# Output projection of a hybrid attention and retention layer: seven block products for eight

## Chip, core and metric

The kernel runs on one core of one Trainium2 chip. The metric is the device time of one execution in microseconds (us). The engines are named as in the profile: PE (TensorE, matmuls), PEld (its weight loads), DVE (VectorE), ACT (ScalarE), POOL (GpSimd) and SP (SyncE, which issues nearly all DMAs).

## What is computed

```python
h = rms_norm(x, norm_gain)                       # x: 1 x 2048 x 1024
proj = jnp.einsum('bsd,de->bse', h, w_in)        # 1024 -> 5632 columns
aq, ak, av, ag, rq, rk, rv, rg = jnp.split(proj, SPLIT_POINTS, axis=-1)
attn = window_attention(aq, ak, av, q_gain, k_gain, sinks)
ret = retention(rq, rk, rv, ret_norm_gain)
mixed = jnp.concatenate([attn * silu(ag), ret * silu(rg)], axis=-1)
x = x + jnp.einsum('bse,ed->bsd', mixed, w_out)  # 2048 -> 1024 columns
```

All matrices are float32. The last line is the output projection, and it is the part of which this document tells.

## The kernel before

**Units.** The rows are cut into four blocks of 512 and the heads into four groups. One group in one block is a unit n, from 0 to 15. Each unit has "jobs", each of which fills one PSUM bank. There are three job banks, taken in turn, so a job may start when the job three before it has been read out (`bank_free`, L1410).

- Q jobs 0 to 3 make query, key and value for a tile of 128 rows each (384 columns, 24 matmuls).
- G jobs 4 to 7 make the attention gate, and the retention's query and key (512 columns, 24 matmuls each).
- V jobs 8 to 11 make the retention's value and gate (512 columns, 24 matmuls each).
- O jobs 12 to 19 are the output projection: four row tiles t by two halves h of 512 output columns, each over the unit's 512 mixed features (four slices k of 128). A job has 4 x 3 = 12 matmuls of 128x128 on 512 columns, since every operand is a pair of a rounded high and a low part, and high x high, high x low and low x high are summed (L1469 to L1471). The O jobs of unit n-1 run inside unit n, between its Q and G jobs. In the last unit they stand behind V(15), and those of unit 15 at the very end.

Between jobs PE runs the small attention and retention steps: TQ, S_, PT, PV, A, I and MT. MT(n,t) transposes the finished retention tile; `mth` on ACT (L696) and `mtl` on DVE (L910) write its high and low part. `mixh` on ACT and `mixl` on POOL (L421) do that for the attention tile. `add` on DVE (L1152) adds each O job's bank to `acc`, which starts as x and is stored at the end of each block. The retention tile itself goes through `gna` and `gnv` (DVE L1111 to L1121), a power on POOL (L435), `gnm` (DVE L1125), `gnx` (ACT L569) and `gnb` (DVE L1132).

**Weights.** They stand in two buffers of 8 x 512 columns, a high one (wH) and a low one (wL). Four panels (Q, G, V, O) go through them in turn, each in four chunks of two k slices. In the first four units a chunk is loaded into a staging buffer, ACT copies it rounded (`wh1`, L541), POOL subtracts (`wl1`, L396), and SP saves both parts to DRAM. The other 12 units reload both parts, a whole panel at a time, as soon as the panel two before it is used up (SP L254).

**Order.** Each engine has its own list of calls written out by hand, and works in order. Nothing is reordered on the chip.

## Time and profile before

| | us |
|---|---|
| median of 3 runs | 1573.88 |
| lowest and highest | 1573.47 and 1574.04 |
| span of the profiled execution | 1571.6 |
| PE busy in it | 1552.0 |
| DVE, ACT, POOL busy | 1124.6, 833.3, 457.9 |

The span runs from the first to the last instruction of one profiled execution. The median is 2.3 us above it, so a change worked out on the span is set off against 1571.6 us, and 2.3 us are put on again for the time. PE is busy in 99% of the span, so first its work counts, then what makes it wait. Its matmuls overlap in the records: one is recorded as 0.39 us long, while the next begins 0.23 us after it.

### The profile page before, as it was taken

What the parts mean: (1) busy time and instruction counts of PE and PEld (TensorE: products, weight loads), DVE (VectorE), ACT (ScalarE), POOL (GpSimd) and SP (SyncE); (2) the same over time, 40 slices, a digit from 0 to 9 for tenths busy, and PEclk for the clock granted to TensorE, in tenths of its full rate; (3) what the DMA queues carried; (4) which work ended last, traced back from release to release, by engine and by line L of the source; (5) the groups of instructions that cost most, each with busy time, mean ns of one, the idle gap of its engine ahead of it and who ended that gap; (6) DMA issues with size and microseconds to landing.
All of it is one profiled execution on the core that took longest, in us unless ns stands there. A gap on an engine that the chain in (4) does not pass through costs nothing.

```text
span 1571.6 us, 24771 instructions
## 1 busy us (share of the span) xinstructions
PE 1552.0 (99%) x8120; PEld 1355.1 (86%) x8120; DVE 1124.6 (72%) x2874; ACT 833.3 (53%) x2331; POOL 457.9 (29%) x453
## 2 busy tenths in 40 slices
...
PEclk9999999999999999999999999999999999999999
...
GB/s 319 308 287 310 155 334 215 269 210 212 296 258 197 161 177 183 165 236 125 215 206 208 250 140 186 211 97 249 172 158 281 146 207 191 140 191 137 174 212 54
DMA packets 123327, 323.65 MB, mean 206 GB/s; under 512 B 16832, under 2 KB 60224, under 8 KB 123200
## 3 DMA queue, kind: packets, MB, share of 16 engines
...
q14 instruction: 61, 0.50, 0.1%
...
## 4 chain that ended last, share of the span: by engine, by line
PE 92%; DVE 4%; POOL 1%; DMA 1%; issue 1%; ACT 1%; SPq 0%; DVEq 0%; ACTq 0%; POOLq 0%
PE jb L1469 26%; PE jb L1470 26%; PE jb L1471 26%; PE ob L1528 2%; PE s L1504 2%; PE ptb L1513 2%; PE ob L1488 1%; PE s L1567 1%; PE ab L1578 1%; PE s L1566 1%; POOL wL L396 1%; PE s L1405 1%; DMA stage<-wp_dram 1%; PE ab L1405 0%; PE ab L1407 0%
## 5 line engine op out<-in xcount | busy, mean ns | idle before, releaser
L1469 PE MATMUL jb<-wH,hTH 128*128 128x512 f32 (+1 forms) x1024 | 376.3, 367 | 13.0 <-POOL wL L396 10.7
L1470 PE MATMUL jb<-wL,hTH 128*128 128x512 f32 (+1 forms) x1024 | 372.6, 364 | 0.0
L1471 PE MATMUL jb<-wH,hTL 128*128 128x512 f32 (+1 forms) x1024 | 372.3, 364 | 0.0
L1469 PEld LDWEIGHTS jb<-wH,hTH 128*128 128x128 f32 x1024 | 193.0, 188 | 33.6 <-POOL wL L396 12.4
L1471 PEld LDWEIGHTS jb<-wH,hTL 128*128 128x128 f32 x1024 | 193.1, 189 | 20.4
L1470 PEld LDWEIGHTS jb<-wL,hTH 128*128 128x128 f32 x1024 | 193.3, 189 | 17.9
L1469 PE MATMUL jb<-wH,mxH 128*128 128x512 f32 x512 | 207.1, 405 | 0.9 <-ACT rawqn L550 0.6
L1469 PE MATMUL jb<-hTH,wH 128*128 128x512 f32 x512 | 201.4, 393 | 0.0
L1471 PE MATMUL jb<-wH,mxL 128*128 128x512 f32 x512 | 200.6, 392 | 0.0
L1470 PE MATMUL jb<-wL,mxH 128*128 128x512 f32 x512 | 200.5, 392 | 0.0
L1470 PE MATMUL jb<-hTL,wH 128*128 128x512 f32 x512 | 200.0, 391 | 0.0
L1471 PE MATMUL jb<-hTH,wL 128*128 128x512 f32 x512 | 199.7, 390 | 0.0
L599 ACT ACTIVATE sx<-sx,nm 128x128 f32<-128x128 f32 x256 | 99.8, 391 | 166.1 <-DVE d L1001 166.0
L421 POOL TENSOR_TENSOR mxL<-mixr,mxH 128x256 fp32r<-128x256 f32 x64 | 48.8, 762 | 449.8 <-ACT mxH L661 449.1
L396 POOL TENSOR_TENSOR wL<-stage,wH 128x512 fp32r<-128x512 f32 (+1 forms) x126 | 159.5, 1291 | 63.8 <-ACT wH L541 63.7
L403 POOL TENSOR_TENSOR rstd<-ms,mhalf 128x5 f32<-128x5 f32 x64 | 75.9, 1186 | 134.3 <-DVE ms L943 134.2
L1471 PEld LDWEIGHTS jb<-wH,mxL 128*128 128x128 f32 x512 | 96.2, 188 | 21.1
L1471 PEld LDWEIGHTS jb<-hTH,wL 128*128 128x128 f32 x512 | 96.2, 188 | 20.5
L1469 PEld LDWEIGHTS jb<-hTH,wH 128*128 128x128 f32 x512 | 96.3, 188 | 18.9 <-ACT rawqn L550 0.3
L1469 PEld LDWEIGHTS jb<-wH,mxH 128*128 128x128 f32 x512 | 96.4, 188 | 18.2 <-ACT rawqn L550 0.8
L1470 PEld LDWEIGHTS jb<-hTL,wH 128*128 128x128 f32 x512 | 96.3, 188 | 18.3
L1470 PEld LDWEIGHTS jb<-wL,mxH 128*128 128x128 f32 x512 | 96.6, 189 | 16.6
...
## 6 DMA issues: line engine op xcount, KB each, us to landing
wH<-scrH SPq DMA_DIRECT2D x144, 512.0 KB, 7.0
wL<-scrL SPq DMA_DIRECT2D x144, 512.0 KB, 7.9
stage<-wp_dram SPq DMA_DIRECT2D x48, 512.0 KB, 6.7
scrH<-wH SPq DMA_DIRECT2D x48, 512.0 KB, 6.9
scrL<-wL SPq DMA_DIRECT2D x48, 512.0 KB, 7.8
...
out_dram<-acc SPq DMA_DIRECT2D x16, 512.0 KB, 3.0
```

The source lines that it names most:

```text
L396: pool.tensor_tensor(wL[b][:, s, 0:w], stage_of(at // 2, w)[:, s % 2], wH[b][:, s, 0:w].bitcast(F32), ALU.subtract).then_inc(S["s_wl"], 1)
L403: pool.tensor_tensor(rstd[:, t % 2], ms[:, t % 2], mhalf[:, 0:5], ALU.pow).then_inc(S["s_rstd"], 1)
L421: pool.tensor_tensor(mxL[:, 0:2, cols], mixr[:, :, :], mxH[:, 0:2, cols].bitcast(F32), ALU.subtract).then_inc(S["s_mixl"], 1)
L599: act.activation(v, v, ACT.Exp, bias=nm4[:, t % 2, i:i + 1], accum_out=den[:, t % 2, i:i + 1])
L1405: pe.matmul(o, lh, rh_, start=i == 0, stop=False)
L1469: pe.matmul(o, lh, rh_, start=i == 0, stop=False)
L1470: pe.matmul(o, lh, rl_, start=False, stop=False)
L1471: m = pe.matmul(o, ll, rh_, start=False, stop=i == last)
L1488: m = pe.transpose(tr[:, c * P:(c + 1) * P], qn[:, t % 2, c * P:(c + 1) * P], ident[:, :])
L1504: m = pe.matmul(s_parts[:, par, hp], qS[:, t % 2, 2 * hp + par], kHL[:, :, win], start=True, stop=True)
L1513: m = pe.transpose(ptb[:, i * P:(i + 1) * P], sx[:, at:at + P], ident[:, :])
L1528: m = pe.matmul(o, v, pT[:, par * 256:(par + 1) * 256].rearrange("p (r q) -> p r q", q=64), start=i == 0, stop=i == 1)
```

## The change

**Seven products.** The O work of a unit is a product of two 2 x 2 block matrices: rows 0 to 255 and 256 to 511, against features of attention and retention, against columns 0 to 511 and 512 to 1023. The change forms it by seven block products P1 to P7 in place of eight, and sums of blocks before and after. A product has two halves of 128 rows, and each half is one job of two k slices, that is 6 matmuls. There are 14 O jobs a unit (12 to 25), 84 matmuls in place of 96. P2, P4 and P3 go on in the bank in which P1, P5 and P7 stand.

**Sums of the mixed operand.** POOL and ACT form four more operands a unit out of the mixed tiles (now kept as mix0 and mix1): s3a, s3l, s1l, s2a, s2l, s4a (two instructions) and s4l on POOL, each 512 columns; sh 1 to 4 on ACT. `mixh` and `mixl` are left for two of four tiles. DVE adds the turned retention tile into mix1 (L1392) for two tiles a unit.

**Sums of the weights.** In the first four units DVE forms four sums of weight blocks (`wtw`, 1024 columns each) and three low parts (`wld`), and POOL four low parts (`wlo`). The O panel so has seven chunks of 1024 columns where it had four.

**Output.** acc is changed by two subtractions before (`ini`) and two behind (`fin`) in each block, on POOL, 1024 columns each; in the last block `fiz` on DVE does the second, in four parts of 512. There are 14 `add` a unit for 8. Stores and refills of acc move from SP's queue to ACT's, but for the last block's stores.

**Other moves.** The weights go chunk by chunk through a ring of seven places (a Q panel takes three); a place is loaded when its chunk's last matmul is done, and raw weights land in the low ring itself. O jobs come in pairs between the Q and G jobs. For blocks 1 to 3, `xl` (8 a block, 512 columns) moves from DVE to POOL.

Jobs of a middle unit n, where the two digits are product and half of unit n-1; before, all eight O jobs stood between Q3 and G0:

```diff
+WOVEN = "Q0 Q1 10 11 Q2 20 21 Q3 50 51 G0 40 41 G1 70 71 G2 30 31 G3 60 61 V0 V1 V2 V3".split()
+CARRIED = {2: 1, 4: 5, 3: 7}
+OPERAND = {1: 0, 2: 1, 4: 2, 5: 0, 6: 3, 7: 4, 3: 1}
+OUT_CHUNK = {1: 0, 2: 1, 5: 2, 6: 3, 4: 4, 7: 5, 3: 6}
...
+    tail = [(0, 1, 0), (0, 1, 1), (0, 6, 0), (0, 2, 0), (0, 2, 1), (0, 6, 1), (0, 5, 0), (0, 5, 1), (0, 7, 0), (0, 4, 0), (0, 4, 1),
+            (0, 3, 0), (0, 7, 1), (1, 1, 0), (1, 1, 1), (0, 3, 1), (1, 2, 0), (1, 2, 1), (1, 5, 0), (1, 5, 1), (1, 6, 0), (1, 4, 0),
+            (1, 4, 1), (1, 7, 0), (1, 7, 1), (1, 6, 1), (1, 3, 0), (1, 3, 1)]
...
 def job(n, j):
-                    t, h = (j - J_OUT) // 2, (j - J_OUT) % 2
-                    pairs = [((mxH[:, k, cols], mxL[:, k, cols]), (W[:, 4 * h + k, :], L[:, 4 * h + k, :]))
-                             for k in range(4)]
+                    prod, half = product_of(j)
+                    name, value = {1: ("s_mixl", nth(n, 2, half)), 2: ("s_mtl", nth(n, 4, half)), 4: ("s_mtl", nth(n, 4, 2 + half)),
+                                   5: ("s_s1l", n + 1), 6: ("s_s2l", n + 1), 7: ("s_s3l", n + 1), 3: ("s_s4l", n + 1)}[prod]
+                    pe.wait_ge(S[name], value)
+                    pairs = [((mxH[:, at, half, k], mxL[:, at, half, k]), (hi(chunk)[:, k], lo(chunk)[:, k])) for k in range(2)]
...
 def mth(n, t):
-                    act.wait_ge(S["s_job"], JOB_DONE[n - 1, J_OUT + 2 * t + 1])
+                    act.wait_ge(S["s_job"], product_done(n - 1, 3 if t < 2 else 4))
...
+            def ini(b, i):
+                if b:
+                    pool.wait_ge(s_ai[3], 16 * b)
+                    pool.wait_ge(s_ai[1 + i], 16 * b)
+                else:
+                    pool.wait_ge(S["s_xsq"], NT)
+                    for t in range(2 * (1 - i), NT):
+                        pool.wait_ge(s_first[t], 16)
+                difference(i, S["s_ini"])
```

POOL's order from the start. wL is `wl1`, xr and rstd are powers for the norms. Before:

```order
L396 TENSOR_TENSOR wL<-stage,wH 128x384 x6
L396 TENSOR_TENSOR wL<-sx,wH 128x384 x2
L396 TENSOR_TENSOR wL<-stage,wH 128x512
L441 TENSOR_TENSOR xr<-xm,mhalf 128x2
L396 TENSOR_TENSOR wL<-stage,wH 128x512 x6
L441 TENSOR_TENSOR xr<-xm,mhalf 128x2 x2
L403 TENSOR_TENSOR rstd<-ms,mhalf 128x5
```

And now:

```order
L560 TENSOR_TENSOR wL<-wraw,wH 128x384 x8
L685 TENSOR_TENSOR xr<-xm,mhalf 128x2
L577 TENSOR_TENSOR rstd<-ms,mhalf 128x5
L685 TENSOR_TENSOR xr<-xm,mhalf 128x2 x2
L560 TENSOR_TENSOR wL<-wraw,wH 128x512
L577 TENSOR_TENSOR rstd<-ms,mhalf 128x5
L560 TENSOR_TENSOR wL<-wraw,wH 128x512
L649 TENSOR_TENSOR acc<-acc 128x2x512
L560 TENSOR_TENSOR wL<-wraw,wH 128x512 x2
L685 TENSOR_TENSOR xr<-xm,mhalf 128x2
L560 TENSOR_TENSOR wL<-wraw,wH 128x512 x4
```

The first G panel's subtractions now stand behind two powers for the first tile, and six of the eight behind the subtraction on acc (`ini`), which waits until ACT has squared all four row tiles.

DVE's order in unit 2, where the O jobs of unit 1 are added. Before:

```order
L1152 TENSOR_TENSOR acc<-acc,jb 128x512
L1132 SCALAR_TENSOR_TENSOR oraw<-oraw,xr,gg 128x256
L1152 TENSOR_TENSOR acc<-acc,jb 128x512
L956 TENSOR_TENSOR rawqn<-rawqn,rstd 128x320
L959 TENSOR_TENSOR rawqn<-rawqn,rstd 128x64
L968 SCALAR_TENSOR_TENSOR qS<-ob,qkg,qS 64x4x64 x2
```

And now:

```order
L1403 TENSOR_TENSOR wraw<-stage 128x1024
L1408 TENSOR_TENSOR stage<-stage,wraw 128x1024
L1410 TENSOR_TENSOR stage<-stage 128x1024
L1430 TENSOR_TENSOR acc<-acc,jb 128x512
L1392 TENSOR_TENSOR mix<-mix,ab 128x256
L1153 TENSOR_TENSOR mxL<-ab,mxH 128x256
L348 TENSOR_TENSOR wL<-wraw,wH 128x1024
L1430 TENSOR_TENSOR acc<-acc,jb 128x512
L1212 SCALAR_TENSOR_TENSOR qS<-ob,qkg,qS 64x4x64 x2
L1217 SCALAR_TENSOR_TENSOR kHL<-ob,qkg,kHL 128x128
L1413 TENSOR_TENSOR stage<-stage 128x1024
```

Five instructions of 1024 columns stand among the additions and the attention's steps, where there were none.

POOL's order at the end. mxL is the low part of an O operand, gnf the power in the last retention tile's norm. Before:

```order
L435 TENSOR_TENSOR gnf<-ve,mhalf 128x2
L421 TENSOR_TENSOR mxL<-mixr,mxH 128x2x128
L435 TENSOR_TENSOR gnf<-ve,mhalf 128x2
L421 TENSOR_TENSOR mxL<-mixr,mxH 128x2x128 x2
L105 UNCONDITIONAL_BRANCH
```

And now:

```order
L603 TENSOR_TENSOR mxraw<-mix 128x512
L608 TENSOR_TENSOR mxL<-mxraw,mxH 128x512
L679 TENSOR_TENSOR gnf<-ve,mhalf 128x2
L621 TENSOR_TENSOR mix<-mix 128x512
L613 TENSOR_TENSOR mxL<-mix,mxH 128x512
L626 TENSOR_TENSOR mxL<-mix,mxH 128x512
L634 TENSOR_TENSOR mix<-mix,mxH 128x512
L637 TENSOR_TENSOR mix<-mix,mxL 128x512
L642 TENSOR_TENSOR mxL<-mix,mxH 128x512
```

Behind the last power stand six instructions of 512 columns; L613 is `s1l`, for which PE's P5 of unit 15 waits, and `s2a` (L621) stands ahead of it.

## Rows read from the trace of the kernel before

**Rows 1.** The page of the profile: span, busy time, PE clock in tenths
```profile
span 1571.6 us, 24771 instructions
PE 1552.0 (99%) x8120; PEld 1355.1 (86%) x8120; DVE 1124.6 (72%) x2874; ACT 833.3 (53%) x2331; POOL 457.9 (29%) x453
PEclk9999999999999999999999999999999999999999
```

**Rows 2.** Windows by unit (0, 1, 2, 8, last): length, busy us, clock, DMA share, GB/s
```profile
59.80:162.46 102.66, 100.41 (x534) 87.36 (x533) 91.36 (x201) 67.67 (x188) 63.80 (x56) 1.00 0.75 270
162.46:259.65 97.19, 97.19 (x514) 85.10 (x513) 76.14 (x182) 60.05 (x159) 59.71 (x55) 1.00 0.69 259
259.65:356.79 97.14, 97.14 (x514) 85.10 (x513) 75.49 (x172) 58.42 (x155) 57.24 (x52) 1.00 0.59 215
842.45:938.75 96.30, 96.30 (x506) 84.28 (x505) 64.33 (x173) 49.46 (x144) 17.47 (x19) 1.00 0.49 180
1491.54:1571.60 80.06, 76.25 (x380) 64.11 (x378) 45.26 (x116) 25.02 (x68) 10.97 (x14) 1.00 0.35 132
```

**Rows 3.** Waits of PE over the span: total us, times, longest
```profile
PE jb L1469 <- POOL wL L396: 10.7, 3, 9.9
PE jb L1469 <- DVE hTL L910: 2.2, 2, 1.9
```

**Rows 4.** Timeline of PE, O jobs at the end: start, length; first and last of 60
```profile
1554.03 0.39 PE L1469 MATMUL jb<-wH,mxH 128*128 128x512 f32 x1
...
1567.41 0.39 PE L1471 MATMUL jb<-wH,mxL 128*128 128x512 f32 x1
```

**Rows 5.** Groups by shape: busy us, mean ns of one, idle before
```profile
L396 POOL TENSOR_TENSOR wL<-stage,wH 128x512 fp32r<-128x512 f32 x96 | 127.6, 1355 | 52.8 <-ACT wH L541 52.8
...
L1152 DVE TENSOR_TENSOR acc<-acc,jb 128x512 f32<-128x512 f32 x128 | 87.4, 683 | 25.9 <-PE jb L1471 24.4
...
L910 DVE TENSOR_TENSOR mxL<-ab,mxH 128x256 fp32r<-128x256 f32 x64 | 26.7, 418 | 0.2
...
L696 ACT ACTIVATE mxH<-ab 128x256 fp32r<-128x256 f32 x64 | 23.8, 371 | 23.8 <-PE ab L1578 23.8
```

**Rows 6.** Two DVE groups of one size by tile: ns min/median/max
```profile
L910 DVE TENSOR_TENSOR hTL<-xt,hTH x30: 678/685/1766, 17.9 to 1168.3; 128x512 fp32r<-128x512 f32 x30
...
L910 DVE TENSOR_TENSOR pTL<-ptb,pTH x64: 678/684/693, 64.3 to 1538.1; 128x512 fp32r<-128x512 f32 x64
```

**Rows 7.** DMA issues: size, median us from issue to landing
```profile
wL<-scrL SPq DMA_DIRECT2D x144, 512.0 KB, 7.9
stage<-wp_dram SPq DMA_DIRECT2D x48, 512.0 KB, 6.7
...
out_dram<-acc SPq DMA_DIRECT2D x16, 512.0 KB, 3.0
```

**Rows 8.** Timeline of PE at the start: jobs 2, 3 and 4
```profile
26.54 0.34 PE L1469 MATMUL jb<-wH,hTH 128*128 128x384 f32 x1
...
29.09 0.41 PE L1469 MATMUL jb<-wH,hTH 128*128 128x384 f32 x1 [1.88 <-DVE hTL L910]
...
33.52 0.50 PE L1469 MATMUL jb<-hTH,wH 128*128 128x512 f32 x1
```

**Rows 9.** Timeline of DVE at the end: a retention tile's norm, the last addition
```profile
1531.40 0.23 DVE L1121 TENSOR_SCALAR ve<-mv,xe 128x2 f32<-128x2 f32 x1
...
1533.62 0.49 DVE L1132 SCALAR_TENSOR_TENSOR oraw<-oraw,xr,gg 128x256 f32<-128x256 f32 x1 [0.34 <-ACT oraw L569]
...
1534.75 0.42 DVE L1111 TENSOR_TENSOR oraw<-oraw,s 128x256 f32<-128x256 f32 x1
...
1536.01 0.23 DVE L1121 TENSOR_SCALAR ve<-mv,xe 128x2 f32<-128x2 f32 x1
...
1567.83 0.69 DVE L1152 TENSOR_TENSOR acc<-acc,jb 128x512 f32<-128x512 f32 x1 [2.03 <-PE jb L1471]
```

More of the change, by code:

```diff
@@ new lines, in ring_places @@
+def ring_places():
+    free, places = [0] * SLOTS, []
+    for n, p, c in CHUNKS:
+        size = 2 * W_WIDTH[p]
+        if p == 0 and c:
+            places.append((places[-1][1], places[-1][1] + size))
+        elif p == 0:
+            at = min(range(SLOTS - 2), key=lambda i: (max(free[i:i + 3]), i))
+            free[at:at + 3] = [last_use((n, p, 3))] * 3
+            places.append((1024 * at, 1024 * at + size))
+        else:
+            at = min(range(SLOTS), key=lambda i: (free[i], i))
+            free[at] = last_use((n, p, c))
+            places.append((1024 * at, 1024 * at + size))
+    return places
@@ new lines, with released @@
+EARLY_AT = {k: i for i, k in enumerate(EARLY)}
+def released(chunk):
+    n, p, c = chunk
+    if p == 3:
+        return "s_job", max(JOB_DONE[n, OUT_JOB[i, q]] for i in OUT_CHUNK if OUT_CHUNK[i] == c for q in range(2))
+    if c < 3:
+        return "s_rel", EARLY_AT[chunk] + 1
+    return "s_job", JOB_DONE[n, PANEL_LAST[p]]
+PLAIN = [k for k in CHUNKS if k[0] < NU and k[1] < 3]
+PLAIN_AT = {k: i for i, k in enumerate(PLAIN)}
+RAW = [k for k in CHUNKS if k[0] < NU and (k[1] < 3 or k[2] in (1, 6))]
@@ L195, in build @@
         s_w = [S["s_w0"], S["s_w1"], S["s_w2"]]
+        s_rw = [S[f"s_rw{i}"] for i in range(LANES)]
         s_xt = [S["s_xt0"], S["s_xt1"]]
@@ new lines, in s4l, with difference @@
+            def s4l(n):
+                pool.wait_ge(S["s_s4h"], n + 1)
+                pool.tensor_tensor(flat(mxL[:, 1]), flat(mix1[:, :, :, :]), flat(mxH[:, 1]).bitcast(F32), ALU.subtract
+                                   ).then_inc(S["s_s4l"], 1)
+            def difference(i, done):
+                left, right = acc[:, :, 0:512], acc[:, :, 512:1024]
+                to = left[:, 2:4] if i == 0 else right[:, 0:2]
+                pool.tensor_tensor(to, right[:, 2:4], to, ALU.subtract).then_inc(done, 1)
@@ new lines, in _ @@
+            s4a(11); s4l(11); rql(12); mixl(12, 0); rkl(12); mixl(12, 1); fin(2, 0); fin(2, 1); ggm(12, 0); s3a(12)
+            s3l(12); ggm(12, 1); ini(3, 0); ini(3, 1); gpow(12, 0); ggm(12, 2); gpow(12, 1); ggm(12, 3); rpow(13, 0)
+            gpow(12, 2); rpow(13, 1); gpow(12, 3); s2a(12); s1l(12); rpow(13, 2); s4a(12); s2l(12); s4l(12)
+            rpow(13, 3); mixl(13, 0); rql(13); mixl(13, 1); rkl(13); ggm(13, 0); s3a(13); s3l(13); ggm(13, 1)
+            gpow(13, 0); ggm(13, 2); gpow(13, 1); ggm(13, 3); gpow(13, 2); rpow(14, 0); rpow(14, 1); gpow(13, 3)
@@ new lines, in quarter, with rows_of, store @@
+            def quarter(whole, q):
+                return whole[:, 2 * (q % 2):2 * (q % 2) + 2, q // 2 * 512:q // 2 * 512 + 512]
+            def rows_of(whole, b, q):
+                at = b * BLK + q % 2 * 2 * P
+                return whole[0, at:at + 2 * P, q // 2 * 512:q // 2 * 512 + 512].rearrange("(t p) d -> p t d", p=P)
+            def store(b, q):
+                last = NU * b + NU - 1
+                if q in (0, 3):
+                    act.wait_ge(S["s_acc"], added(last, (2,) if q == 0 else (1, 5, 6, 7)))
+                else:
+                    act.wait_ge(S["s_fin"], 2 * b + q)
+                act.dma_start(rows_of(out, b, q), quarter(acc, q)).then_inc(s_st[q], 16)
```

1554 lines of the change are left out of this document (868 added, 686 removed).

## The prediction

> **What bounds the kernel now.** I read the page first: PE is busy 1552.0 of 1571.6 us at full clock [rows 1]. Then the windows by unit: from unit 1 on PE is busy in the whole of each window, while DVE fills 76.14 of 97.19 us in unit 1 and 64.33 of 96.30 in unit 8 [rows 2]. Then PE's waits: 10.7 us on POOL's wL and 2.2 on hTL [rows 3], both in the first 30 us, and nothing worth naming later. So the middle is bound by PE's own work. Matmuls taken out count in full there, and waits put in count too, because there are none to hide behind.
>
> **What is removed.** 12 matmuls of 512 columns in each of 16 units, 192 in all. A record's length (0.39 us) overlaps the next, so the price is the spacing: 60 matmuls in a row start from 1554.03 to 1567.41, 13.38 us in 59 steps, 0.2268 us each [rows 4]. 192 x 0.2268 = **43.5 us** off, 2.72 a unit. Six matmuls make a job of 1.36 us. A job starts in that same spacing, so six more jobs a unit cost PE nothing by these rows. All terms below are PE's waits, put on again.
>
> **The end: +7.5.** This is the term I trust most, since the order has nothing between. P3 of unit 14 reads its operand where `mth` for tiles 0 and 1 of unit 15 must write. P3's last half, job(14,23), now stands behind P1 of unit 15, and right behind it PE has MT(15,1).
> - MT(15,1) needs the bank of MT(15,0) read: `mth` 0.37 and `mtl` 0.42 after job(14,23) [rows 5]. PE idles 0.9 us with a hop.
> - MT(15,3) needs the last tile's norm. ACT copies that tile only behind `mth` of tile 1: 0.37 + about 0.37 for the copy (of `mth`'s size), then 1.26 from `gna` to `ve` (1534.75 to 1536.01) and 2.71 from `ve` to the end of `gnb` (1531.40 to 1534.11) [rows 5, 9], 4.7 us. PE has two jobs and a transpose of about 0.25 for it, 3.0. It idles 1.7, with DVE's additions in between about 2.
> - P5 of unit 15 stands right behind MT(15,3) and waits for `mth` 0.37, the addition 0.42, `s2a` 1.36 and `s1l` 1.36 [rows 5], with four hops 3.9.
> - Behind the last matmul comes `add` and now a `fiz` of 0.68 [rows 5, 9]: 0.7.
> Sum 7.5, and 5 to 10 as its bounds. `s4l` has 8 jobs, 10.9 us, for six POOL and ACT steps; it hides.
>
> **The start: +2.** Job 2 ends at about 27.1 (its last three matmuls start at 26.54 [rows 8]). Then ACT evicts (1.3) and squares the fourth tile (1.05), and `ini` runs 2 x 1.355: until 32.2. POOL then has two low parts (2.7), the power that the transposes XB ahead of job 4 wait for (0.7): 35.6. Four more low parts end at 41.0, and job 4 with them at 41.5, where it started at 33.52 and took 5.5 [rows 8], so ended at 39.1. XB's and TQ's 0.9 us came after that. So 1.5 to 2.4 late. Bounds: 0, as POOL was late there already [rows 3], and 6 if both `ini` count.
>
> **Units 1 to 3: +9.** Two things come together, counted once.
> - DVE: 75.5 us of unit 2 are filled [rows 2]. To it come 6 `add` (4.1), 2 additions for mix1 (0.84) and 7 instructions of 1024 columns at twice 0.684 (9.6) [rows 5, 6]: 90.0 of a unit of 97.14 - 2.72 = 94.4. POOL's load grows from 57 to about 71 (8 + 8 more instructions' worth less what goes), and with 40 us more of POOL work DVE's same 172 instructions took 11 us longer than in unit 8 [rows 2], so 14 more give 3.8: 93.8, or 99%. At 89% in unit 0 PE lost 2.25 us [rows 2], at 78% in unit 1 nothing.
> - V panel: its first place comes free 12.2 us before V0 (G3, four O jobs and A). Loading takes 6.7 by the median, 3.0 by the store that has the queues to itself [rows 7], ACT 0.6, then POOL eight low parts, one of rk and a `mixl`, 12.9: ready 8.0 or 4.3 us after V0 starts, where its last slice is wanted at 4.8. So 0 to 3.2 us.
> I take 3 us in each of three units. The bounds are 0 and 6.5 a unit, the latter for a DVE that reaches 93%: 93.8 / 0.93 = 100.9.
>
> By the Trainium skill (SBUF — State Buffer, Who interferes with whom) a DVE instruction with two SBUF inputs and a GpSimd instruction that reads SBUF exclude each other for a whole instruction. That speaks against this change, which gives both more of them. The trace agrees: hTL with two SBUF inputs ranges from 678 to 1766 ns, pTL with one in PSUM only from 678 to 693 [rows 6]. By the rule each of the seven new ones could wait out one low part of 1355 ns, up to 9.5 us a unit more; the sum with 9.5 in place of 3 in three units would be some 19 us above mine.
>
> **The other units: +1.5.** The ACT, POOL and DVE work grows, but DVE has 32 us idle in unit 8 and POOL 79 [rows 2], and some 5 and 9 us are added. The tightest chain is MT(n,3), `mth`, addition, `s2a`, `s1l`, then P5: 3.9 us beside a P2 half, Q3 and S_, 6.1 us, of which DVE's and ACT's queues take some. Banks: the job behind a pair has 2.7 us for the eviction of the one before it, 0.7 on DVE or 0.6 on ACT. Block changes put `fin` and `ini`, 10.8 us, on POOL. Bounds 0 and 12. No gain is possible from the moved `xl` or refills, since PE waits for none of them now.
>
> **The sum.** 1571.6 - 43.5 + 7.5 + 2 + 9 + 1.5 = 1548.1 of span, and with 2.3 around it **1550.4**; I say 1550.
>
> **Rivals.**
> - *The covers hold* (0.20). Only the end costs: 1571.6 - 43.5 + 7.5 + 2.3 = 1538. For it: PE never waited in units 1 and 2 at 78% DVE. Against it: 95 to 99% is another matter.
> - *DVE and POOL bound the first block* (0.20). 6.5 us a unit in place of 3, and 3 more in unit 0 or 4: 1550 + 13.5 = 1564. By the skill's lock above it would be more, to 1569.
> - *The ring's leads fail in every later unit* (0.06): slower than before. The last G chunk of a unit takes the place of a Q chunk that is free at half of Q3. To its use are left 12 matmuls of Q (2.1), two O jobs (2.7), 18 of G (4.1) and two small steps (0.9): 9.8 us, the last V chunk about the same. The panel before had a whole panel's time. wL lands 7.9 us after issue by the median [rows 7], with the issue 8.4, so 1.4 is left. Loads that come 3 us later lose 1.6 at two or three places, and with the raised traffic (a unit reloads 18.9 MB for 15.7, three O chunks more) maybe 2 at each: 5.5 a unit, 66 in 12 units, 1616. It decides from 1.9 us a unit, that is from landings of some 10.3. Against it: 7.9 is for eight issued in a burst, here they come in pairs, and DMA is busy only 49% [rows 2].
> - *Short products gain less* (0.04). If each O job cost 0.1 us at its head, 96 more jobs cost 10: 1560.
>
> **How the numbers follow.** The forecast has 0.50, with a range of its own of 1543 to 1558. A measurement tells about 0.2%, 3.1 us, from no change. Slower than 1577.0 is only the ring's case: 0.05. Within: 0.02 from the thin ends of the rivals. Faster: 0.93. The range from 1536 to 1566 takes in the first two rivals and the short products, about 0.85.
>
> **What would show it.** PE's records must fall by 192 and a middle unit last 93.6 us, not 96.3. PE must wait for `s1l` (POOL mxL L613) once by about 4 us some 18 us before the end, and for the acc subtraction's successors near 35 us. Units 1 to 3 would last about 97, and DVE be at 93% or more there. Wrong it would be if middle units stay above 95, with PE waiting for DMA wH or wL (the ring), or if units 1 to 3 last 94.4 (the covers hold) or over 100.

## The result

The kernel after the change takes 1643.17 us (median of 4 runs, 1641.58 to 1645.9), the kernel before 1573.68 beside it: a ratio of 1.0443, with a 95% interval of 1.0428 to 1.0458. It is 69.5 us slower, where 1550 and a gain had been forecast. The matmuls went away as planned, 192 of them. In the profiled execution, the longest of the four (1645.9 us, a span of 1643.9), the kernel is 72.3 us behind, so 115.8 us of new loss stand against 43.5 us saved; by the medians it is 113.0.

The page of the kernel after, in the lines that answer to [rows 1]:

```profile
span 1643.9 us, 25336 instructions
PE 1548.5 (94%) x7928; PEld 1333.7 (81%) x7928; DVE 1321.2 (80%) x3010; ACT 866.0 (53%) x2359; POOL 678.2 (41%) x571
PEclk9999999999999999999999999999999999999998
```

PE was busy in 99% of the span and is so in 94%. DVE's busy time has grown by 197 us, POOL's by 220. By the prices of the forecast DVE's new instructions come to about 100 us (14.5 us in each of four units and 4.9 in the other twelve, less 16 for `xl`). The mean granted clock is 0.984 of full.

Where the time went is read best by stretches that hold the same jobs in both kernels. Units are cut at the first matmul of Q0. Windows of the kernel after, with the columns of [rows 2]: unit 0, units 1 to 4, units 5 to 14, unit 15 with the end:

```profile
9.33:98.24 88.91, 81.00 (x402) 69.70 (x402) 79.03 (x158) 57.46 (x151) 58.74 (x49) 0.96 0.75 286
98.24:540.23 441.99, 397.95 (x1993) 338.37 (x1992) 390.77 (x753) 236.59 (x604) 263.88 (x197) 0.97 0.71 260
540.23:1511.65 971.42, 951.21 (x4947) 825.35 (x4946) 753.91 (x1864) 510.37 (x1437) 315.22 (x283) 1.00 0.59 216
1511.65:1643.87 132.22, 118.31 (x593) 100.24 (x591) 92.31 (x230) 56.42 (x159) 35.84 (x34) 0.97 0.54 197
```

And the same stretches before:

```profile
9.89:88.43 78.54, 74.59 (x372) 63.27 (x372) 66.41 (x138) 54.80 (x145) 54.87 (x48) 1.00 0.88 329
88.43:483.62 395.19, 393.27 (x2085) 344.24 (x2083) 310.76 (x733) 229.82 (x615) 198.24 (x180) 1.00 0.66 244
483.62:1446.56 962.94, 962.94 (x5044) 842.53 (x5043) 664.26 (x1785) 490.86 (x1407) 183.49 (x198) 1.00 0.51 186
1446.56:1571.60 125.04, 121.23 (x628) 105.03 (x626) 79.07 (x214) 54.19 (x158) 19.88 (x22) 1.00 0.42 155
```

Take the length before, less 2.72 us for each unit's removed matmuls (none in unit 0, which has no O work yet, and 5.4 in the last stretch, which has that of two units), from the length after. The loss is 9.8 us up to unit 1, counted from the start of the span, **57.7 in units 1 to 4**, **35.7 in units 5 to 14** and 12.7 in unit 15 and the end. (The counts show that up to 44 short matmuls, some 5 us, changed sides at a cut, so the first and third loss are a little too large and the second too small.)

No single wait stands out. PE's waits over the whole span, in us, times and longest (compare [rows 3]):

```profile
PE jb L1737 <- DVE hTL L1463: 9.3, 1, 9.3
PE jb L1737 <- issue: 8.7, 3, 3.5
PE ob L1758 <- DVE kHL L1217: 8.3, 7, 2.4
PE ab L1848 <- DVE oraw L1382: 6.7, 7, 2.9
PE ptb L1783 <- DVE sx L1254: 6.0, 7, 1.6
PE jb L1737 <- DVE acc L1430: 5.2, 2, 2.8
PE ab L1859 <- POOL xr L685: 4.6, 1, 4.6
...
PE jb L1737 <- POOL wL L560: 3.4, 6, 1.1
PE jb L1737 <- DMA wL<-scrL: 3.4, 4, 1.5
```

Only the first is the start-up that the kernel before had too (9.9 us there, put down to POOL's wL). Most others name DVE, each time another of its results, and each is 1 to 3 us long. That is the picture of an engine that is late as a whole.

**Why DVE is late.** Two stretches of the same 6 us in unit 2. First POOL, then DVE (start, length):

```profile
246.36 1.30 POOL L634 TENSOR_TENSOR mix<-mix,mxH 128x512 f32<-128x512 f32 x1
247.73 1.29 POOL L637 TENSOR_TENSOR mix<-mix,mxL 128x512 f32<-128x512 f32 x1
248.98 1.29 POOL L626 TENSOR_TENSOR mxL<-mix,mxH 128x512 fp32r<-128x512 f32 x1
250.23 2.39 POOL L348 TENSOR_TENSOR wL<-stage,wH 128x1024 fp32r<-128x1024 f32 x1
```

```profile
247.29 0.69 DVE L1240 TENSOR_REDUCE m<-sx 128x4 f32<-128x512 f32 x1
248.01 1.03 DVE L1243 SCALAR_TENSOR_TENSOR nm<-m,nsink 128x4 f32<-128x4 f32 x1
249.07 1.22 DVE L1245 TENSOR_TENSOR d<-nm,sink 128x4 f32<-128x4 f32 x1
250.21 0.48 DVE L1186 TENSOR_REDUCE ss<-th 128x5 f32<-128x320 f32 x1
250.72 1.93 DVE L1187 TENSOR_SCALAR ms<-ss 128x5 f32<-128x5 f32 x1
```

nm, d and ms work on 4 or 5 columns and take 0.16, 0.16 and 0.17 us at their shortest. Here each ends when the POOL instruction beside it ends: nm at 249.04 (POOL 249.02), d at 250.29 (250.27), ms at 252.65 (252.62). The two TENSOR_REDUCE are not stretched. Three of POOL's added instructions turned 0.5 us of DVE's work into 4.2. The same by tile: aL (128x256, two SBUF inputs), shortest, median and longest in ns, before and after ([rows 6] had hTL):

```profile
L910 DVE TENSOR_TENSOR aL<-amr,aH x64: 410/419/1505, 77.4 to 1528.0; 128x256 fp32r<-128x256 f32 x64
```

```profile
L1153 DVE TENSOR_TENSOR aL<-amr,aH x64: 409/419/2617, 77.3 to 1590.1; 128x256 fp32r<-128x256 f32 x64
```

For the whole kernel I add up, over all DVE instructions, the length less the shortest of the same line and shape, and call that the **excess**. It was 95 us before and is 212 after: 51 and 99 in units 1 to 4, 23 and 85 in units 5 to 14. (Finer or coarser groups of shapes move each of these by up to 6 us.) Not all of the growth lies beside POOL's new instructions: `rqL`, which POOL formed before too, now stands beside DVE's `mix` (64x256), 14 of 80 of which take over 0.9 us in units 5 to 14 where it was 2, some 11 us of excess.

**The clock.** In unit 2, timeline of PE (start, length), and then windows around it (the granted clock is the last figure but two):

```profile
278.67 0.39 PE L1739 MATMUL jb<-wH,mxL 128*128 128x512 f32 x1
282.31 0.30 PE L1810 MATMUL ab<-ident,kr 128*128 128x128 f32 x1 [3.26 <-issue]
...
284.61 0.63 PE L1737 MATMUL jb<-wH,mxH 128*128 128x512 f32 x1
285.03 0.63 PE L1738 MATMUL jb<-wL,mxH 128*128 128x512 f32 x1
...
287.08 0.39 PE L1737 MATMUL jb<-wH,mxH 128*128 128x512 f32 x1
```

```profile
274.00:278.60 4.60, 4.60 (x27) 4.01 (x27) 4.50 (x16) 4.11 (x14) 2.50 (x4) 1.00 0.99 380
...
283.00:287.00 4.00, 4.00 (x13) 3.25 (x14) 3.92 (x6) 2.62 (x11) 4.00 (x4) 0.57 1.02 418
```

PE stood for 3.26 us, and for the next 4 us its matmuls came every 0.43 us in place of 0.23, at 0.57 of the full clock, near the lower of its two levels (1.2 GHz). Behind the start-up there are seven waits of 2.5 us or more, and six of them lie in or right beside such a stretch; other stretches follow groups of shorter waits. By the spacing, the matmuls in them cost 17.9 us over full speed in the whole kernel; the same count gives 2.5 before, where the clock was full up to the last matmul. PE is busy for 46.2 us at the low level, half of which, 23 us, is the most that it can have cost. So some 15 to 23 of the 115.8 us, an estimate, are not waits but what waits cause.

The rest is waiting: PE's idle time grew from 19.6 to 95.4 us, in 88 waits for 10. Each wait also hides some 0.16 us behind the recorded end of the matmul before it (0.39 us long at a spacing of 0.23), which makes another 12 us by estimate.

### The profile page after: what moved, and what is told of

It is laid out like the page before. It is cut to its first block, busy times and chain, and to the rows that moved or that the text cites. A ratio compares the mean times of both kernels' runs of the same rounds, so it can differ in the third digit from the quotient of the medians.

```text
span 1643.9 us, 25336 instructions
## 1 busy us (share of the span) xinstructions
PE 1548.5 (94%) x7928; PEld 1333.7 (81%) x7928; DVE 1321.2 (80%) x3010; ACT 866.0 (53%) x2359; POOL 678.2 (41%) x571
## 4 chain that ended last, share of the span: by engine, by line
PE 47%; DVE 15%; issue 4%; DMA 2%; ACT 1%; POOL 1%; SPq 0%; DVEq 0%; POOLq 0%; ACTq 0%
PE jb L1737 14%; PE jb L1738 13%; PE jb L1739 13%; DMA wL<-scrL 2%; PE ob L1798 1%; DVE acc L1430 1%; DVE aL L1153 1%; DVE rst L1352 1%; PE ptb L1783 1%; DVE rst L1153 1%; PE s L1774 1%; DVE oraw L1359 1%; DVE qS L1212 1%; PE s L1836 1%; DVE kwL L1153 1%
## 5 line engine op out<-in xcount | busy, mean ns | idle before, releaser
L1737 PE MATMUL jb<-wH,hTH 128*128 128x512 f32 (+1 forms) x1024 | 376.9, 368 | 10.4 <-DVE hTL L1463 9.3
L1737 PE MATMUL jb<-wH,mxH 128*128 128x512 f32 x448 | 186.9, 417 | 20.1 <-issue 8.7
L1738 PE MATMUL jb<-wL,mxH 128*128 128x512 f32 x448 | 179.6, 401 | 0.0
L1739 PE MATMUL jb<-wH,mxL 128*128 128x512 f32 x448 | 179.2, 400 | 0.0
L1430 DVE TENSOR_TENSOR acc<-acc,jb 128x512 f32<-128x512 f32 x224 | 152.4, 681 | 21.8 <-PE jb L1739 18.4
L560 POOL TENSOR_TENSOR wL<-wraw,wH 128x512 fp32r<-128x512 f32 (+1 forms) x96 | 124.6, 1319 | 44.2 <-ACT wH L756 43.9
L1737 PEld LDWEIGHTS jb<-wH,mxH 128*128 128x128 f32 x448 | 86.6, 193 | 37.0 <-issue 17.1
L584 POOL TENSOR_TENSOR rqL<-th,rqH 64x512 fp32r<-64x512 f32 x32 | 42.4, 1326 | 179.1 <-ACT zst L854 162.1
L679 POOL TENSOR_TENSOR gnf<-ve,mhalf 128x2 f32<-128x2 f32 x64 | 47.9, 748 | 163.9 <-DVE ve L1371 163.9
L1738 PEld LDWEIGHTS jb<-hTL,wH 128*128 128x128 f32 x512 | 96.7, 189 | 19.2
```

The costliest lines, as they stand in the source:

```text
L560: pool.tensor_tensor(lo(chunk)[:, s % 2], raw_lo(chunk)[:, s % 2], hi(chunk)[:, s % 2].bitcast(F32), ALU.subtract).then_inc(S["s_wl"], 1)
L584: pool.tensor_tensor(rqL[rows, a], th[rows, :], rqH[rows, a].bitcast(F32), ALU.subtract).then_inc(S["s_rql"], 1)
L679: pool.tensor_tensor(gnf[:, t % 2, 0:2], ve[:, :], mhalf[:, 0:2], ALU.pow).then_inc(S["s_grs"], 1)
L1430: v.tensor_tensor(a, a, bank_of(n, J_OUT + i)[:, :], ALU.add).then_inc(S["s_acc"], 1)
L1737: pe.matmul(o, lh, rh_, start=begins and i == 0, stop=False, **go_on)
L1738: pe.matmul(o, lh, rl_, start=False, stop=False, **go_on)
```

## The experiments

Theory A: POOL's added instructions read SBUF and stretch DVE's. Rival B: the ring and the order of the jobs. Rival C: DVE's own added instructions. Rival D: what was added holds POOL's queue, and what stands behind it is late. All kernels made from the kernel after stand side by side. Medians are of two or three runs each (four of the kernel after); single runs of one kernel differ by 0.5 to 8 us, the two of sums_filled by 14. The losses are those of the profiled run, by the stretches above, in us; that run was the slower one in some, 1616.8 us in sums_filled and 1600.9 in all_pool_paced.

| kernel | median us | ratio to before, 95% | to unit 1 | 1 to 4 | 5 to 14 | 15, end | excess 1 to 4 | 5 to 14 |
|---|---|---|---|---|---|---|---|---|
| after the change | 1643.2 | 1.0443 (1.0428 to 1.0458) | 9.8 | 57.7 | 35.7 | 12.7 | 99 | 85 |
| sums_filled | 1609.8 | 1.0231 (1.0125 to 1.0337) | 9.3 | 44.6 | 22.6 | 10.3 | 78 | 50 |
| weight_sums_filled | 1603.3 | 1.0190 (1.0160 to 1.0219) | 8.6 | 18.0 | 32.3 | 13.7 | 65 | 102 |
| both_filled | 1591.6 | 1.0116 (1.0083 to 1.0148) | 7.4 | 21.0 | 24.3 | 11.0 | 53 | 65 |
| reload_half | 1636.1 | 1.0396 (1.0366 to 1.0427) | 8.4 | 55.6 | 28.2 | 12.7 | 96 | 87 |
| ini_fin_short | 1631.8 | 1.0370 (1.0330 to 1.0409) | 7.7 | 51.6 | 27.0 | 12.8 | 94 | 80 |
| adds_half | 1632.1 | 1.0371 (1.0341 to 1.0401) | 9.2 | 51.3 | 29.7 | 11.9 | 94 | 87 |
| pool_low_filled | 1623.7 | 1.0321 (1.0291 to 1.0351) | 9.1 | 33.5 | 36.3 | 12.8 | 73 | 88 |
| pool_low_paced | 1623.7 | 1.0317 (1.0287 to 1.0347) | 10.0 | 40.0 | 29.7 | 13.0 | 76 | 82 |
| dve_weight_filled | 1630.8 | 1.0367 (1.0337 to 1.0397) | 10.8 | 41.1 | 37.4 | 13.2 | 92 | 103 |
| sums_paced | 1615.7 | 1.0266 (1.0236 to 1.0295) | 8.3 | 42.0 | 21.8 | 12.2 | 72 | 46 |
| sums_on_dve | 1662.8 | 1.0565 (1.0527 to 1.0603) | 8.6 | 57.7 | 55.4 | 13.2 | 97 | 50 |
| low_on_dve | 1644.0 | 1.0446 (1.0415 to 1.0476) | 9.2 | 56.5 | 36.0 | 13.4 | 74 | 82 |
| all_pool_paced | 1594.9 | 1.0145 (1.0112 to 1.0178) | 8.7 | 29.6 | 19.2 | 13.3 | 49 | 37 |
| pool_paced_dve_filled | 1588.9 | 1.0106 (1.0086 to 1.0126) | 5.8 | 21.5 | 21.7 | 13.9 | 48 | 54 |
| all_short | 1563.8 | 0.9943 (0.9921 to 0.9966) | 5.8 | 8.9 | 10.4 | 8.5 | 53 | 66 |

The last column can't be compared for the five kernels in which DVE's weight sums are filled. There a few additions of units 1 to 3 take 0.62 us in place of 0.67 to 0.69, and as the shortest of their kind they lift the excess of all others. Counted from the fastest tenth of each kind, units 5 to 14 have 81 us in the kernel after and 23 in the kernel before, and 78 in weight_sums_filled, 44 in both_filled, 81 in dve_weight_filled, 33 in pool_paced_dve_filled and 43 in all_short.

**sums_filled.** The eight instructions for the operand sums become fills of the same tiles, for example:

```diff
 def s1l(n):
     pool.wait_ge(S["s_s1h"], n + 1)
-    pool.tensor_tensor(flat(mxL[:, 0]), flat(mix1[:, :, :, :]), flat(mxH[:, 0]).bitcast(F32), ALU.subtract
+    pool.memset(flat(mxL[:, 0]).bitcast(F32), 0.0001
                        ).then_inc(S["s_s1l"], 1)
```

> The kernel after the change, but the eight instructions of POOL that form the sums of the mixed operand and their low parts only write a constant over the same tiles, and read nothing; every wait and every other instruction stays. (The sums are left out, so the products are of other numbers.) Theory A, POOL's reading of SBUF stretches DVE's instructions with two SBUF inputs, and DVE's late results stop PE: the time that DVE's instructions take over the shortest of their kind falls from 4 to 12 us a unit to about 3 in units 5 to 14, these units lose 2 to 3 us less each, units 1 to 4 some 2 to 4 less, and the kernel takes 1595 to 1615 us in place of 1643. Rival B, the order of jobs and the ring of weights make PE wait: nothing of that changes, 1635 to 1643. Rival C, only DVE's own added instructions matter: these are all still there, 1635 to 1643 too, but with DVE's excess down.

1609.8 us, 33 less, in the range of theory A; its two runs, 1602.8 and 1616.8, lie on both sides. In the profiled one, the slower, units 1 to 4 and 5 to 14 gained 13 us each, and the excess fell in both.

**weight_sums_filled** and **both_filled.** The same for `wtw`, `wld` and `wlo`; then both edits.

```diff
-    v.tensor_tensor(t1, b12, b11, ALU.subtract).then_inc(S["s_twin"], 1)
+    v.memset(t1, 0.01).then_inc(S["s_twin"], 1)
...
-    return engine.tensor_tensor(lo(chunk), src, hi(chunk).bitcast(F32), ALU.subtract)
+    return engine.memset(lo(chunk).bitcast(F32), 0.00001)
```

> The kernel after the change, but the four sums of weights a unit, and the seven low parts of the output weights (three on DVE, four on POOL), only write a constant, in units 0 to 3; waits stay. (The weight sums and those low parts are left out.) They are 8.5 us of DVE and 10.8 us of POOL in each of four units. Theory A or C (DVE is full in the first five units, 91 to 93 percent): units 1 to 4, which last 108.2, 111.7, 109.4 and 112.8 us, come to 98 to 103, and the kernel to 1605 to 1615. Rival B (the V panel's chain, the order and the ring): units 1 to 4 keep at least 105, 1630 or more. Units 5 to 15 must not change under any theory.

> Both edits of the two runs before together (sums of operands and of weights and their low parts only write constants). Theory A: the two gains add or do better, 1560 to 1580, with units 1 to 3 near 97 and units 5 to 14 near 94. Rival C: as the weight sums alone, 1605 to 1615. Rival B: 1625 or more, and then what is left of PE's waits names the place.

The weight sums cost 40 us, nearly all of it in units 1 to 4; 1603.3 is 2 us below the range of theories A and C. Both together gave 52 and not 73: 1591.6 is above what I gave to theory A and below all that I gave to the others. The two overlap in units 1 to 4, and some 60 us of loss do not come from either.

**Three other loads, one at a time.** reload_half, ini_fin_short and adds_half:

```diff
-    sp.dma_start(dst.bitcast(F32), src[:, c]).then_inc(s_ld[i % LANES], 16)
+    sp.dma_start(dst[:, 0].bitcast(F32), src[:, c, 0]).then_inc(s_ld[i % LANES], 16)
```

```diff
-    pool.tensor_tensor(to, right[:, 2:4], to, ALU.subtract).then_inc(done, 1)
+    pool.tensor_tensor(to[:, :, 0:32], right[:, 2:4, 0:32], to[:, :, 0:32], ALU.subtract).then_inc(done, 1)
```

```diff
-    v.tensor_tensor(a, a, bank_of(n, J_OUT + i)[:, :], ALU.add).then_inc(S["s_acc"], 1)
+    v.tensor_tensor(a[:, 0:256], a[:, 0:256], bank_of(n, J_OUT + i)[:, 0:256], ALU.add).then_inc(S["s_acc"], 1)
```

> The kernel after the change, but each reload of a chunk in units 4 to 15 brings only the first of its two k slices, half of the bytes, through the same waits. (The second slice keeps older weights.) Rival B, the ring's leads are too short: PE's waits for DMA wL (3.4 us in all by the trace) and what follows them vanish, and more than that if late weights also hide behind other waits, 5 us or more off in units 5 to 14, 1620 to 1638. Theory A (DVE is late, the ring is only touched): at most 4 us off, 1638 to 1643.

> The kernel after the change, but the subtractions on acc at the start and end of each block (ini and fin on POOL) cover 32 of 512 columns. (Most of acc is so not prepared.) They are 2.7 us of POOL each, two before block 0 and four at each of three block changes. Theory D, they hold POOL's queue: the 4.6 us that PE waits for the first tile's power near 34 us fall to 1 or less, and with it 3 to 5 us of the start; units 4, 8 or 9, 12 or 13 lose 1 to 4 us less each; 1625 to 1636. If the start is late by POOL's low parts anyway: 1640 to 1643.

> The kernel after the change, but each of the 14 additions a unit covers 256 of its bank's 512 columns. (Half of the output is not added.) DVE so spends 14 x 0.27 = 3.8 us less a unit, less than the eight additions cost before the change. An addition reads one operand from PSUM. Theory C, the count and length of DVE's instructions matter: 3 to 4 us less in each of units 1 to 4 and 1 to 2 in the others, 1610 to 1625. Theory A, the stretching by POOL matters more than the own load: units 5 to 14 gain under 1 us each, units 1 to 4 gain 2 to 3, 1625 to 1637.

Halved reloads gave 7 us, so rival B is true, but small. The low parts of the weights land 7.4 us after issue in the kernel after, by the median ([rows 7]: 7.9):

```profile
wL<-scrL SPq DMA_DIRECT2D x180, 512.0 KB, 7.4
```

PE's four waits for DMA wL (3.4 us) lie in units 4, 6, 7 and 10, three of them at an O job behind the first G job. The short ini and fin gave 11 us, 2 of them at the start and the rest around the block changes, and the halved additions 11, spread over all units, as theory A had it.

**What POOL's added work costs the kernel before.** It got eight more POOL instructions a unit in units 6 to 15, for which nobody waits:

```diff
+    def extra():
+        pool.tensor_tensor(more[:, 512:1024], more[:, 0:512], more[:, 0:512], ALU.subtract).then_inc(S["s_mhalf"], 1)
...
-    ...; rpow(6, 2); gpow(5, 3); rpow(6, 3); xpow(2, 0); xpow(2, 1)
+    ...; rpow(6, 2); extra(); extra(); extra(); extra(); extra(); extra(); gpow(5, 3); rpow(6, 3); xpow(2, 0); xpow(2, 1)
```

> The kernel before the change, and in units 6 to 15 eight more instructions of POOL a unit, 512 columns with two SBUF inputs, two behind the second gg and six behind the third rstd, where the changed kernel has its operand sums; no other engine waits for them (result unchanged). Theory A: DVE's excess over the shortest instruction of each kind rises from 2.2 us a unit to 5 to 9 there, with DVE's own count the same; PE has slack for most of it in this kernel, so 0 to 10 us more in all. A price per instruction of POOL of 0.4 to 0.8 us of DVE comes out. If POOL and DVE do not hinder each other: DVE's busy time in units 6 to 14 stays within 0.5 us, and the kernel's time too.

It took 1596.5 us (ratio 1.0147, 1.0117 to 1.0176), 22.9 more than the kernel before, where I had given 0 to 10. The excess rose by only 2 us a unit, and theory A's row of 5 to 9 us did not come. PE's waits tell which power was late, the fourth one of `rpow`, which now stood behind six instructions:

```profile
PE ob L1500 <- DVE kHL L985: 17.2, 18, 1.3
```

The next kernel has the six behind that power.

```diff
-    ...; rpow(6, 2); extra(); extra(); extra(); extra(); extra(); extra(); gpow(5, 3); rpow(6, 3); xpow(2, 0); xpow(2, 1)
+    ...; rpow(6, 2); gpow(5, 3); rpow(6, 3); extra(); extra(); extra(); extra(); extra(); extra(); xpow(2, 0); xpow(2, 1)
```

> The kernel before the change with the same eight more POOL instructions a unit as in the run named before_pool_sums, which cost 22.9 us though no engine waits for them, but the six of them stand behind the last rstd power of a unit in place of ahead of it. If they cost by POOL's queue (the power for the fourth tile's key and query is late, so kHL is, for which PE waited 17.2 us there): 1574 to 1577. If they cost by stretching DVE: 1585 to 1597 as before. DVE's excess should be 4 us a unit in both cases.

1575.8 us (ratio 1.0014, 1.0003 to 1.0025), with the same excess, and the row is

```profile
PE ob L1500 <- DVE kHL L985: 1.9, 2, 1.0
```

That is rival D, pure: the same instructions cost 22.9 us at one place of POOL's queue and 2.3 us at another. Then eight instructions a unit on DVE were added as well, one of their places being:

```diff
+    def more_dve():
+        link(v.tensor_tensor(more[:, 1024:1536], more[:, 0:512], more[:, 0:512], ALU.subtract))
...
-    ...; part2(7, 0); tql(7, 2); ...
+    ...; part2(7, 0); more_dve(); tql(7, 2); ...
```

> The kernel before the change with the eight POOL instructions a unit of the run before_pool_sums_later, and in units 6 to 15 eight more instructions on DVE too, 512 columns with two SBUF inputs, one behind each of the four softmax steps and one behind each mixing step; no other engine waits for any (result unchanged). Both engines then carry in units 6 to 14 more than in the changed kernel (DVE 74 to 80 us at its shortest against 69 to 77). If load and contention are what cost the changed kernel 3.6 us a unit there: units of 98 to 101 us, 1595 to 1620. If it is rather where things stand in the queues and the ring: under 1 us a unit, 1575 to 1585.

1580.3 us (ratio 1.0041, 1.0022 to 1.0061), 6.9 more, 0.7 a unit, where the kernel after loses 3.6 a unit. But its load is not that of the kernel after. In units 6 to 14 DVE's own work, its busy time less the excess, is 68.9 us a unit and 67.0 in the kernel after, so it has a little more; POOL is busy for 27.0 us and not 31.9, ACT for 49.0 and not 51.3, the excess is 5.0 and not 9.0, and nobody waits for what was added. The run shows that DVE's own work alone does not explain units 5 to 14. It does not part the order from the contention and from the chains that pass through the new instructions.

**Stretching or queue, in the kernel after.** First one half of the weight sums at a time.

```diff
+    if c not in LOW_ON_DVE:
+        return engine.memset(lo(chunk).bitcast(F32), 0.00001)
     return engine.tensor_tensor(lo(chunk), src, hi(chunk).bitcast(F32), ALU.subtract)
```

> The kernel after the change, but the four low parts of weight sums that POOL forms in each of units 0 to 3 only write a constant; DVE's seven instructions stay. (Those low parts are left out.) Both kinds together gave 40 us. If the stretching of DVE by POOL's reads is what fills DVE (theory A), this half gives 12 to 25 us, with DVE's excess in units 1 to 4 down by 3 or more each: 1618 to 1631. If it is DVE's own instructions and their place in its queue (theory C), at most 8: 1635 to 1643.

> The kernel after the change, but the four sums and three low parts of weights that DVE forms in each of units 0 to 3 (1024 columns each) only write a constant; POOL's four low parts stay. (Those sums are left out.) Theory C: this half gives 28 to 40 of the 40 us of both, 1603 to 1615. Theory A: 15 to 28, 1615 to 1628.

POOL's four low parts a unit (16 in all, about 2.4 us each) cost 19.5 us, DVE's 28 instructions only 12.4: the first is in theory A's range, the second 3 us above it. So DVE's own work is the smaller part of what the weight sums cost. The fills are shorter than the sums (0.96 us for 1024 columns), so this does not yet tell theory A from rival D. The two runs named paced do. There each sum is filled two and a half times over, so that POOL is held as long, and reads nothing:

```diff
-    out_low(pool, n, c).then_inc(S["s_olp"], 1)
+    low = lo((n, 3, c)).bitcast(F32)
+    out_low(pool, n, c)
+    pad(low)
+    pad(low)
+    pool.memset(low[:, 0], 0.00001).then_inc(S["s_olp"], 1)
```

> As the run pool_low_filled (POOL's four low parts of weight sums a unit, in units 0 to 3, only write constants; 20 us faster), but each now writes its constant two and a half times over, so that it holds POOL for the 2.4 us that the low part took, and reads nothing. If the 20 us came from POOL's reads stretching DVE (theory A), they stay: 1620 to 1628. If they came from POOL's queue (powers and low parts of weights behind them came earlier): 1638 to 1645.

> As the run sums_filled (the eight operand sums and low parts a unit on POOL only write constants; 33 us faster), but each writes for the 1.3 us that the sum took, and reads nothing. Theory A: the 33 us stay but for the few of the end's chain, 1608 to 1618. POOL's queue (in the kernel before, six more instructions ahead of one power cost 23 us, behind it 2): most of them go, 1630 to 1643.

(Here `out_low` only waits.) The low parts: 1623.7 us with short fills and 1623.7 with long ones. The operand sums: 1609.8 and 1615.7. So by medians of two runs each the 19.5 us and some 27 of the 33 us come from POOL's reads. In the stretch of units 1 to 4 the split is less clean (24 us off with short fills, 18 with long ones), and the 6 us between 1609.8 and 1615.7 are less than sums_filled differs from itself. Then everything that POOL was given was made long fills (sums, low parts, ini and fin, hTL of blocks 1 to 3), and after that DVE's weight sums fills too:

> The kernel after the change with all that it gave POOL replaced by constants written for as long as the work took, reading nothing: the operand sums, the four low parts of weight sums, ini and fin, and the eight hTL of blocks 1 to 3. (All of these are left out.) POOL's busy time and queue stay, DVE's instructions too. The sums alone gave 27 us, the low parts 20. Theory A (reads stretch DVE): 1643 less 47 less 5 to 15 for the rest, 1580 to 1592, and DVE's excess in units 5 to 14, 4 to 12 us, near 1 to 3. If POOL's queue at the block changes (ini, fin) cost the rest: 1592 to 1600.

> The run before, and DVE's four weight sums and three low parts a unit in units 0 to 3 only write constants too. That gave 12 us alone. If DVE's length and its stretching make one load on the same engine, it gives 8 to 16 on top: 1568 to 1580. If DVE has room once it is not stretched, under 4: 1578 to 1590, and the rest is the order's.

1594.9 us, 48 less than the kernel after, at nearly its POOL and all of its DVE work. That is above the 1580 to 1592 of theory A and in the range that I had given to POOL's queue at the block changes, 1592 to 1600; the single runs (1593.0, 1594.9, 1600.9) touch both. So the reads of `ini`, `fin` and `hTL` added little to the some 47 us of sums and low parts. Its page:

```profile
PE 1533.1 (96%) x7928; PEld 1327.8 (83%) x7928; DVE 1211.7 (76%) x3010; ACT 866.9 (54%) x2359; POOL 672.9 (42%) x935
```

POOL is busy 672.9 us, as it was (678.2), and DVE has the same 3010 instructions, yet 110 us less of them. The excess in units 1 to 4 is 49, what it was before the change, and in units 5 to 14 it is 37 for 23, 11 us of it again `mix` beside `rqL`. What the fills still stretch are DVE instructions with one SBUF input (ms, 0.17 us at its shortest, and casts), some 8 us in all; the longest ms, at 29.02, ends with a fill at 30.00:

```profile
L1220 DVE TENSOR_SCALAR ms<-ss x64: 169/171/1008, 19.2 to 1490.8; 128x5 f32<-128x5 f32 x64
```

DVE's weight sums then gave 6 us more, little against the spread of these runs: 1588.9 lies in the range that I had given to a DVE with room (1578 to 1590), where the forecast for one load on one engine was 1568 to 1580.

**Moving the work to DVE.** These two leave nothing out. A piece of POOL's list and one of DVE's, for the operand sums of unit 6 (in low_on_dve the `wlo` calls become `wld` calls likewise):

```diff
-    s2a(6); s1l(6); s2l(6); s4a(6); rpow(7, 3); s4l(6)
+    rpow(7, 3)
...
-    mtl(6, 3); add(6, 3); qk_norm(7, 2); v_parts(7, 2)
+    mtl(6, 3); s2a(6); add(6, 3); s1l(6); qk_norm(7, 2); s2l(6); s4a(6); v_parts(7, 2)
```

> The kernel after the change with the seven operand sums and low parts of units 5 to 13 on DVE in place of POOL (result unchanged). DVE reads two SBUF inputs in 0.6 us where POOL takes 1.3, so the time in which the two exclude each other halves, but DVE's queue is longer by 5 us a unit. Theory A: DVE's excess in units 6 to 13 falls from 4 to 12 us to 2 to 6, and the units gain 0.5 to 1.5 each: 1630 to 1640. Theory C (the length of DVE's queue): 1643 to 1655.

> The kernel after the change with all seven low parts of weight sums on DVE, where POOL formed four (result unchanged). DVE has 4 x 1.2 us more of its own in each of units 1 to 4, POOL 9.6 us less. Theory A: DVE's excess falls by 5 to 6 us a unit, as when POOL's four were only filled, so DVE's busy time stays about level, and the kernel takes 1630 to 1643. Theory C: DVE, the engine that was full, gets 19 us more, and the kernel takes 1650 to 1665.

The low parts on DVE: 1644.0 us, no change. 19 us more of DVE's own work stand against 25 us less excess in units 1 to 4; PE's waits for DVE's wL grew from 3.0 to 13.4 us, and others shrank. The operand sums on DVE: 1662.8 us, where theory A had 1630 to 1640 and even the theory of DVE's queue only 1643 to 1655. The excess in units 5 to 14 fell from 85 to 50 us as forecast, but the units lost 20 us more. In this order a DVE that is stretched less but has 5 us more to do a unit makes PE wait still more.

**All loads taken off together** (all edits of both_filled, reload_half, ini_fin_short and adds_half):

> The kernel after the change with all five loads taken off at once: operand sums and weight sums only write constants, reloads bring one k slice of two, ini and fin cover 32 of 512 columns, additions 256 of 512. What is left above 1538, the time that I gave for a change whose covers hold, is due to the order of the jobs and of each engine's calls alone. The single edits gave 33, 40, 8, 12 and 11 us, 104 in all; the first two together gave 52 and not 73. If they overlap further: 1560 to 1575, some 20 to 35 us are the order's. If each rests on a place of its own: 1545 to 1560.

1563.8 us, within the first range. With all of that work shortened or filled (fills and half additions still take their time), PE still loses 33.6 us of the 43.5 that the seven products save. Its clock is 0.998 of full and by the spacing the low clock costs 4.6 us, where it was 17.9. No kernel here beats the kernel before and computes the whole; the only one below it is this one.

## Why the prediction was wrong

**The 43.5 us were right.** PE has 192 records fewer, and jobs of six matmuls cost nothing at their heads: in unit 6, 264 steps from one of their matmuls to the next take 60.61 us, 0.2296 each, where 274 took 63.07, 0.2302 each. The rival of the short products is out.

**The end was right.** I gave 7.5 us, made of MT(15,1) 0.9, MT(15,3) 2, P5 3.9 and the last fiz 0.7. Timeline of PE, with its waits in brackets:

```profile
1614.46 0.41 PE L1848 MATMUL ab<-ident,oraw 128*128 128x128 f32 x2 [1.20 <-DVE mxL L1153]
...
1619.95 0.44 PE L1848 MATMUL ab<-ident,oraw 128*128 128x128 f32 x2 [2.07 <-DVE oraw L1382]
1623.93 0.77 PE L1737 MATMUL jb<-wH,mxH 128*128 128x512 f32 x1 [3.54 <-issue]
1624.50 0.63 PE L1738 MATMUL jb<-wL,mxH 128*128 128x512 f32 x1
```

1.20, 2.07 and 3.54 us, the last one 20 us before the end, and 0.7 for the last `fiz`. The profile puts the last wait down to "issue", but POOL's row tells whom it waited for, ending at 1623.84:

```profile
1622.57 1.27 POOL L613 TENSOR_TENSOR mxL<-mix,mxH 128x512 fp32r<-128x512 f32 x1
```

What I missed is what follows: at the low clock the next 11 steps take 4.68 us, 2.2 more than at full speed. The stretch lost 12.7 in all; 1.6 us of the rest is a wait for amr.

**The start came out nearly right, in part by luck.** PE waited for POOL's power xr, named in the forecast, and job 4 began at 34.00 (33.52 before, [rows 8]), most of its first ten matmuls at the low clock:

```profile
33.90 0.32 PE L1859 MATMUL ab<-ident,xr 128*128 128x128 f32 x1 [4.63 <-POOL xr L685]
34.00 0.47 PE L1737 MATMUL jb<-hTH,wH 128*128 128x512 f32 x1
34.64 0.63 PE L1739 MATMUL jb<-hTH,wL 128*128 128x512 f32 x1
```

Job 4 ended at 41.3, where I had 41.5, but not for my reason: its last low part was ready at 39.82 and not 41.0, since `ini` began at 28.12, some 1.3 us sooner than I had put it, and it was the low clock (34.4 to 37.8) that held the job. By the first kr eviction the kernel was 1.7 us behind, where I had put 2. Another 8 us were lost up to unit 1, about half of them by work that moved across the cut, and the rest I had not seen.

**Units 1 to 3: the term of the sum that was mis-sized most.** I put 9 us, bounds 0 to 19.5, and nothing for unit 4. Units 1 to 3 lost 41.1 and unit 4 another 16.6. DVE's own instructions I had about right. The step that failed is "14 more give 3.8": from DVE's 11 us more at 40 us more of POOL work I took a rate and scaled it. POOL's load did grow by about that, 16.4 us a unit in units 1 to 4, but the excess grew by 9 to 14 us a unit in place of 3.8. The rate was taken between two units in which DVE had room; and POOL's new work stands in runs of four to six instructions beside DVE's shortest ones; which of the two made the rate so much higher, no run tells. The bound was wrong too, since it asked how full DVE can be made (93%), and not how much later each of its results comes. DVE was at 93% in unit 2 just as foretold (104.02 of 111.66 us), but the unit lasted 112 us, not 97.

The rule of the Trainium skill that I weighed there (SBUF — State Buffer, Who interferes with whom) was the better guide. The trace and all_pool_paced agree with it: two SBUF inputs on DVE against a read on POOL are stretched to the end of POOL's instruction, as nm and d above; long fills in place of the reads take 110 us off DVE's busy time; and an instruction with an input in PSUM stays at its shortest (acc, 670 to 691 ns in all 224). But I applied it to the seven new instructions on DVE alone. All of DVE's old ones with two SBUF inputs meet POOL's new ones too, above all the shortest. The same section of the Trainium skill also says that a `tensor_scalar` can take the shared ports, and ms above, with one input, is such a case: 1.93 us for 0.17, and up to 1.01 beside fills.

**The other units: the "+1.5" failed**, and with it "DVE has 32 us idle in unit 8 and POOL 79" as a cover. Units 5 to 14 lost 35.7 us and unit 4 its 16.6, where the bound for all of them was 12. Idle time as an average of a unit covers nothing if a chain through DVE, ACT and POOL must end beside a given job. Halved reloads, short ini and fin, half additions and filled operand sums each gave 6 to 13 us there: thin covers, and each is a share of the loss. That the order itself is the cause of the rest, 10.4 us in all_short, is argued and not shown: the kernel before bears a DVE with as much work of its own (before_pool_dve) at 0.7 us a unit, and it keeps eight O jobs in a row, while the new order has them in pairs between the jobs whose results the small steps need. But nobody waited for the work added there, and no run changed the order alone, so that stays open.

**The rivals.** The mechanism of "DVE and POOL bound the first block" was the right one, at more than twice its price (14.4 us a unit for 6.5), with later units that it left out. The ring (0.06), the only case on the slower side, came about at its place in small: 7 of the 66 us. The forecast of slower had 0.05, for a reason that gave a tenth of the loss. What was missing was a rival in which lost time itself costs: some 15 to 23 us of it are the clock.

By size, each as a difference of medians to 1643.2, overlaps and all: POOL's reads 48 us, DVE's weight sums 6 more (12 alone), and the reloads, the half additions and the rest of POOL's time 25 more by all_short. What all_short still loses is 33.6 us, and no run says to what.
